# Block kernel on one core: merge loads moved into the SSM stage, the experts' end worked by 128-row blocks with four extra load areas, and the RWKV shift split into single operations

## The chip, the cores and the metric

The program runs on one core of one Trainium2 chip. The time is device microseconds from the start to the end of one execution. Before the change three runs gave a median of 5053.02 us (5052.44 to 5054.24). All arithmetic is fp32.

## What is computed

The reference is a stack of blocks on 512 tokens of width 1024. The first one mixes two branches and is followed by a mixture of experts; two attention blocks come after it. Cut to what matters here:

```python
pl = hl @ w_in; rw, ss, gates = split(pl)          # also for 256 context tokens
ya = rwkv_branch(centred_shift(rw))                # u + mu0*(prev-u) + mu1*(next-u), then two scans
yb = ssm_branch(to_colmajor(ss))                   # conv, two chunked scans, rms_norm over 2048
ga, gb = split(sigmoid(gates))
m  = (ga * (ya @ proj_a) + gb * (yb @ proj_b)) @ w_out
x  = x + g1 * rms_norm(m)
h2 = rms_norm(x) * (1 + sc2) + sh2
x  = x + g2 * rms_norm(ec_moe(h2))                 # 16 experts, each takes its 64 best tokens
for l in range(2):                                 # attention, gates, FFN; first line of each:
    h = rms_norm(x, attn_norm[l]); proj = h @ w_in_2[l]
```

## The kernel before, in words

The program is a row of stages: start, RWKV, SSM, merge, experts (MoE), and two attention blocks (block2). In each stage every engine has its own function (`..._sync` for SP, which issues all DMAs on one queue, `..._tensor` for TensorE, `..._vector`, `..._scalar`, `..._gpsimd`). Engines run in program order and wait for one another by counting semaphores. At a stage's end each engine calls `meet` (L211): it drains, counts up its own line, and waits for the lines of all four compute engines.

**RWKV** works on 8 tiles of 128 channels (j = 0 to 7). What the engines do is set by one list, `b.order`, that `rwkv_order` (L672) makes: eight generators are asked in turn (`turns`, L371), once each in a round, and what they yield is written one behind the other: two lanes (d = 0, 1: triangular inverses of one scan direction each, 16 rounds for two chunks: `tri`, then five `level`/`merge` pairs with `products` between them, `turn_bk`, `corner`, `join`), two steppers (`rest`, `solve`, `update`), the tails, the projector, the chain (decay factors and keys), the modulator. Each engine walks this list and does its share of each step. A lane takes 48 rounds for a tile. The projector yields for tile j: 8 `project` steps for k (i = 1), `shift` steps, 2 `lora` steps, 8 `project` steps for r (i = 2), a `shift` step, `kk_norm`, 8 `project` steps for v (i = 0), `shift` steps, `turn_v` (six transposes), `gate`, 2 `lora` steps. In a `shift` step (L1121) ScalarE first scales the PSUM result in full at part 0 (`shift`, L1338), and VectorE then adds the left and the right neighbour with one `scalar_tensor_tensor` each: two operations for columns 0 to 512 in part 0, two for 512 to 768 (the context) in part 1. In the `corner` step TensorE's result is copied by VectorE (two copies for each lane) and by ScalarE (one), and `join` on TensorE waits for these copies. VectorE's predicated copies of the next `tri` wait for GpSimd to have filled X (`unit`, L1467), and GpSimd's keys stand ahead of that in its order.

**SSM** (`ssm_order`, L1503) ends with 16 `mgate` steps (merge gates: eight matmul pairs each, copied by ScalarE, stored to `gmd` by SP); the tiles of yb go to `ybd` from the `read` steps. Its last work is `yrstd`: VectorE, ScalarE, VectorE, four small matmuls, one copy; then `meet`.

**Merge** (`merge_sync`, L2013): SP waits for the meeting, then loads in order pa 0, yaT (2 MB, from `yad`), pb 0, ybT (4 MB, from `ybd`), gates, pa 1, pb 1 and the rest. TensorE takes pa d and pb d in turn for d = 0 to 7 (8 and 16 matmuls of 128x512, two records each), then the output projection. Weights go through a ring of six areas of 1 MB in `wreg`.

**Experts** (`moe_sync`, L2173): 192 loads of 1 MB through a ring of eight areas, two for each step of the list `todo`; the load for step i waits until TensorE has finished step i - 4. After the last `combine(7)` VectorE adds four 128-row blocks, ScalarE squares all four, VectorE makes one `mvar` for all, ScalarE one Ln and Exp for all, VectorE scales and adds the four blocks; `meet`; then block2 starts with its norm of x (square, variance, Ln, Exp, scale, eight transposes, gain, for each block) and meets once more (`("norm", 0)`). SP issues c2 and the first two weights of block2 (b0a) after the first of these meetings.

## Time and profile before

| | |
|---|---|
| median of 3 runs | 5053.02 us |
| the profiled execution | 5058.15 us |
| its span in the trace | 5056.1 us |
| PE busy / PE weight loads / DVE / ACT / POOL | 91% / 56% / 41% / 26% / 9% |
| granted TensorE clock, mean | 0.954 |
| DMA | 503 MB, mean 100 GB/s; 351 to 408 GB/s in the experts' slices |
| stages in the trace (us) | RWKV 53 to 1214, SSM to 1975, merge to 2225, experts to 2808, block2 to the end |

The busy share of PE is modelled (a matmul's end is not seen), so it says that PE seldom waits, not that it runs at its peak. In rows of the timeline the first number is the start, the second the time from the first to the last of the merged instructions, the brackets tell how long the engine had been idle and what released it. PEclk is the granted clock as a share of 2.4 GHz.

### The profile page before, as it was taken

To read this page: it belongs to the slowest core of one execution; us is meant where nothing else is said; L and a number is where in the kernel's file an instruction comes from. 1 tells how busy PE (TensorE), PEld (TensorE's weight loads), DVE (VectorE), ACT (ScalarE), POOL (GpSimd) and SP (SyncE) were. 2 spreads that over 40 slices of the span, in tenths; PEclk is the share of its full clock that TensorE was granted. 3 is DMA by queue.
4 is the path that set the end of the run, shared out by engine and by line. 5 is a ranking of instruction groups with operands and counts; after the bars stand their busy time and mean duration, and the time that the engine had idled before them with its cause. 6 is when DMAs were issued, how large, how long until landed. Compare 5 with 4: busy or idle time off the path is not lost.

```text
span 5056.1 us, 85351 instructions
## 1 busy us (share of the span) xinstructions
PE 4614.6 (91%) x36404; PEld 2842.8 (56%) x36404; DVE 2087.9 (41%) x3866; ACT 1336.7 (26%) x2486; POOL 431.0 (9%) x385
## 2 busy tenths in 40 slices
PE   7899899988998898979998898989999998999999
PEld 3566666666555553464443544544788544444787
DVE  3554555463355542130111336463343237463333
ACT  2333333332222211010000124251232123242232
POOL 0121111110222230000000000020000000020000
PEclk9998999998999999989999899999999999999999
DMA  6200000000111014318998211013321211113321
GB/s 228 81 19 5 18 19 17 5 26 13 42 46 38 34 73 179 118 76 351 407 408 362 97 62 61 35 59 140 115 86 50 87 62 61 43 56 139 113 100 50
DMA packets 76818, 503.33 MB, mean 100 GB/s; under 512 B 9480, under 2 KB 10008, under 8 KB 34328
## 3 DMA queue, kind: packets, MB, share of 16 engines
q1 hardware_dynamic: 76440, 497.88, 25.6%
q8 instruction: 287, 4.70, 0.4%
q14 instruction: 91, 0.75, 0.0%
HBM read 472.66 MB, written 25.19 MB: 98 GB/s over the span
## 4 chain that ended last, share of the span: by engine, by line
PE 79%; DVE 8%; issue 6%; DMA 3%; ACT 2%; POOL 1%; SPq 0%; PEldq 0%; PEld 0%; DVEq 0%; ACTq 0%; POOLq 0%
PE ps L224 76%; PE ps L227 3%; DMA upper<-in_ew 2%; DVE upper L243 2%; ACT upper L282 2%; DVE upper L259 1%; DVE upper L235 1%; POOL upper L3394 1%; DVE upper L251 1%; DVE lower L235 1%; DVE lower L243 1%; ACT lower L282 0%; DVE upper L239 0%; DMA upper<-ybd 0%; DVE lower L239 0%
## 5 line engine op out<-in xcount | busy, mean ns | idle before, releaser
L224 PE MATMUL ps<-lower 128*128 128x512 f32 (+12 forms) x7024 | 1935.6, 444 | 66.5 <-issue 22.8
L224 PEld LDWEIGHTS ps<-lower 128*128 128x128 f32 (+3 forms) x7024 | 958.9, 188 | 782.8 <-issue 610.0
L224 PE MATMUL ps<-upper 64*64 64x64 f32 (+7 forms) x15552 | 829.9, 258 | 144.3 <-DVE upper L251 46.4
L282 ACT ACTIVATE upper<-ps 128x512 f32<-128x512 f32 (+5 forms) x967 | 444.9, 491 | 1769.1 <-PE ps L224 1300.8
L224 PEld LDWEIGHTS ps<-upper 64*64 64x64 f32 (+4 forms) x15552 | 596.9, 145 | 449.7 <-issue 223.8
L224 PE MATMUL ps<-lower,upper 64*64 64x64 f32 (+6 forms) x7536 | 725.3, 316 | 50.5 <-DMA lower<-in_ada 20.3
L224 PE MATMUL ps<-rounded 128*128 128x512 f32 x3072 | 712.3, 394 | 7.5 <-DVEq L213 7.5
L224 PEld LDWEIGHTS ps<-rounded 128*128 128x128 f32 x3072 | 579.6, 189 | 139.4 <-issue 8.3
L224 PEld LDWEIGHTS ps<-lower,upper 64*64 64x64 f32 (+3 forms) x7536 | 384.3, 145 | 337.8 <-issue 267.1
L282 ACT ACTIVATE upper<-upper 128x256 f32<-128x256 f32 (+12 forms) x695 | 361.9, 529 | 725.1 <-DVE upper L255 186.8
L224 PE MATMUL ps<-upper,lower 128*128 128x512 f32 (+4 forms) x1584 | 482.1, 474 | 26.2 <-DMA upper<-yad 11.7
L224 PEld LDWEIGHTS ps<-upper,lower 128*128 128x128 f32 (+1 forms) x1584 | 248.3, 197 | 248.9 <-issue 230.0
L259 DVE COPY_PREDICATED upper<-lower,ps 128x256 f32<-128x256 uint8 (+2 forms) x576 | 246.2, 457 | 328.6 <-PE ps L224 293.0
L251 DVE COPY upper<-ps 128x64 f32<-128x64 f32 (+9 forms) x423 | 166.8, 404 | 454.0 <-PE ps L224 423.6
L235 DVE TENSOR_TENSOR rounded<-lower,rounded 128x512 fp32r<-128x512 f32 (+2 forms) x136 | 200.8, 1477 | 226.6 <-ACT rounded L282 226.4
L235 DVE TENSOR_TENSOR upper<-upper,ps 128x512 f32<-128x512 f32 (+1 forms) x136 | 108.5, 798 | 450.2 <-PE ps L224 437.2
L282 ACT ACTIVATE rounded<-lower 128x512 fp32r<-128x512 f32 (+2 forms) x136 | 171.7, 1262 | 374.5 <-PE ps L224 239.7
L227 PE MATMUL ps<-lower,upper 128*128 128x128 f32 (+1 forms) x1204 | 189.0, 290 | 83.6 <-ACT upper L282 38.7
L227 PEld LDWEIGHTS ps<-lower,upper 128*128 128x128 f32 (+1 forms) x1204 | 145.3, 147 | 176.3 <-issue 73.6
L282 ACT ACTIVATE lower<-ps 128x512 f32<-128x512 f32 (+1 forms) x174 | 102.2, 592 | 381.2 <-PE ps L224 351.5
L243 DVE SCALAR_TENSOR_TENSOR upper<-ps,lower,upper 128x511 f32<-128x511 f32 (+1 forms) x208 | 130.1, 625 | 134.1 <-ACT upper L282 128.4
L3381 POOL COPY upper<-lower 128x512 f32<-128x512 f32 x8 | 5.0, 631 | 1933.2 <-PE ps L224 1932.5
(81 smaller groups left out, 2139.5 us busy)
## 6 DMA issues: line engine op xcount, KB each, us to landing
lower<-in_ew SPq DMA_DIRECT2D x144, 1024.0 KB, 10.6
upper<-in_ew SPq DMA_DIRECT2D x48, 1024.0 KB, 13.6
lower<-in_b0f SPq DMA_DIRECT2D x16, 2048.0 KB, 8.0
lower<-in_b1f SPq DMA_DIRECT2D x16, 2048.0 KB, 7.9
upper<-in_ada SPq DMA_DIRECT2D x18, 1024.0 KB, 5.4
lower<-in_wrkv SPq DMA_DIRECT2D x8, 1728.0 KB, 7.5
lower<-in_b0g SPq DMA_DIRECT2D x8, 1536.0 KB, 6.7
gad<-upper SPq DMA_DIRECT2D x48, 256.0 KB, 2.0
```

Source lines behind the costliest of these rows:

```text
L224: return self.e.matmul(out, lhsT, rhs, start=start, stop=stop)
L227: return self.e.transpose(out, in_, self.ident[0:n, 0:n])
L235: self.e.tensor_tensor(out, a, b, op).then_inc(line.up(*event), 1)
L243: self.e.scalar_tensor_tensor(out, a, s, b, op0, op1).then_inc(line.up(*event), 1)
L251: self.e.tensor_copy(out, a).then_inc(line.up(*event), 1)
L259: self.e.copy_predicated(out, mask, data).then_inc(line.up(*event), 1)
L282: self.e.activation(out, in_, func, bias=bias, scale=scale, accum_out=accum).then_inc(line.up(*event), 1)
L3381: g.e.tensor_copy(b3[:, :, 0:64], v3(b.kv[:, i, :], 128)[:, :, 0:64]).then_inc(tail.pool.up(), 1)
L3394: g.e.tensor_tensor(y, y, r, SUB).then_inc(o.lane.pool.up("less", *o.u), 1)
```

## The change

Three parts. In the **RWKV** order a `shift` step is one operation of VectorE, so the projector yields 4, 2 and 4 of them where it yielded 2, 1 and 2. In the **merge** the loads for its start are issued from the SSM stage: yaT right after the stores of SSM group 2 (into group 0's memory, which is then free), pa 0 and pa 1 after merge gate 11, pa 2 and pb 0 after gate 15. TensorE leaves the SSM stage without waiting for the others, and takes pa 0, 1, 2, pb 0, pa 3, pb 1, pa 4, ... (`MERGE`). In the **experts** four loads (steps 4 and 5 of `todo`) go into areas that only later hold acc and r1, r2, r3, scr; the two row loads r2, r3 move behind step 11's load; the last blocks' norm is taken in a staggered order by blocks of 128 rows, block2's first norm with it; the meeting `("norm", 0)` goes; block2's first two weights are issued once step 93 of `todo` is done, ahead of the meeting, and c2 behind it.

```diff
@@ rwkv_order, projector
-                    for part in range(2):
+                    for part in range(4):
                         yield once(("shift", j, i, part))
...
-            yield once(("shift", j, 2, 0))
+            for part in range(2):
+                yield once(("shift", j, 2, part))
...
-            for part in range(2):
+            for part in range(4):
                 yield once(("shift", j, 0, part))
@@ rwkv_vector
-            s, e = ((0, 512), (512, 768))[part]
+            s, e = ((0, 512), (512, 768))[part // 2]
             v.wait_ge(P.act, "project", j, i)
...
+            if part % 2 == 0:
+                v.stt(P.dve, out[:, s + 1:e], ps[:, s:e - 1], ...)
+            else:
+                v.stt(P.dve, out[:, s:e - 1], ps[:, s + 1:e], ..., *last)
@@ ssm_sync
+            if name != "mgate" or z[0] < 11:
+                k.ring.load(*next(k.loads))
+            elif z[0] == 11:
+                merge_begin(k, sp)
+                merge_load(k)
+                merge_load(k)
+            else:
+                merge_load(k)
+                merge_load(k)
...
+            if z == [2, 7]:
+                sp.wait_ge(k.tail.act, "square", 2, 3)
+                for line in k.stored:
+                    sp.wait_ge(line)
+                fetch(sp, k.mg.yaT, k.yad.rearrange("k p t -> p k t"), "yaT")
@@ ssm_tensor
-    pe.meet("pe", "ssm")
+    banks.give("yrstd", M.dve, "rb")
+    k.free = free
+    pe.leave("pe", "ssm")
@@ merge
+MERGE = [("pa", 0), ("pa", 1), ("pa", 2)] + [t for d in range(8) for t in ([("pb", d), ("pa", d + 3)] if d < 5 else [("pb", d)])]
@@ moe_sync
+    ring, extra = Ring(sp, b.w, k.wline[4:8] + k.wline[0:4]), Ring(sp, b.extra, [k.line(f"extra{i}") for i in range(4)])
...
-        if i == 4:
+        if i == 12:
+            sp.wait_ge(M.pe, *todo[5])
             fetch(sp, b.r2, k.mrow_bc(5120, 1024), "r2")
             fetch(sp, b.r3, k.row("n2post"), "r3")
...
+            (extra if i in (4, 5) else ring).load(
+                (*key, e), T[name][2 * (2 * g + e) + f][:, 2048 * z:2048 * z + 2048], M.pe, *key)
+    sp.wait_ge(M.pe, *todo[93])
@@ moe_vector, after the last "down"
+    for t in range(9):
+        if t < 4:
+            combine(7, (t,))
+        if 0 <= t - 2 < 4:
+            add(t - 2)
+        if 0 <= t - 4 < 4:
+            norm_scale_vector(k, v, "attn0", t - 4, b.nscr, b.nss)
+        if 0 <= t - 1 < 4:
+            var(t - 1)
+        if 0 <= t - 3 < 4:
+            norm_var_vector(k, v, "attn0", t - 3, b.nss)
+        if 0 <= t - 5:
+            norm_turn_vector(k, v, "attn0", t - 5, ...)
@@ moe_scalar
+    for t in range(7):
+        if t < 4:
+            a.wait_ge(M.dve, "combine", 7, t)
+            a.act(M.act, b.scr, b.acc[:, t, :], AF.Square, "msq", t, accum=b.ss[:, t:t + 1])
+        if 0 <= t - 1 < 4:
+            r = b.ss[:, t - 1:t]
+            a.wait_ge(M.dve, "mvar", t - 1)
+            a.act(M.act, r, r, AF.Ln)
+            a.act(M.act, r, r, AF.Exp, "mrstd", t - 1, scale=-0.5)
+        if 0 <= t - 2 < 4:
+            a.wait_ge(M.dve, "x1", t - 2)
+            norm_square_scalar(k, a, "attn0", t - 2, b.nscr, b.nss)
+        if 0 <= t - 3:
+            norm_rstd_scalar(k, a, "attn0", t - 3, b.nss)
```

**VectorE at the first corner of a tile.** The lanes are at tile 4, the projector at tile 5, i = 0 (v): 128x511 and 128x255 are the shift's operations, the 128x768 one behind it is the chain's `beta`, the COPY rows are the four corner copies, TENSOR_SCALAR 128x768 is the chain's `keys`, COPY_PREDICATED the masks of `tri` and of the next `merge`. Before:

```order
L243 SCALAR_TENSOR_TENSOR upper<-ps,lower,upper 128x511 x2
L243 SCALAR_TENSOR_TENSOR upper<-lower,upper 128x768
L251 COPY upper<-ps 64x256
L251 COPY upper<-ps 64x4x64
L251 COPY upper<-ps 64x256
L251 COPY upper<-ps 64x4x64
L243 SCALAR_TENSOR_TENSOR upper<-ps,lower,upper 128x255 x2
L239 TENSOR_SCALAR upper<-upper,lower 128x768
L259 COPY_PREDICATED upper<-lower,ps 128x256 x8
```

Now:

```order
L247 SCALAR_TENSOR_TENSOR upper<-ps,lower,upper 128x511
L247 SCALAR_TENSOR_TENSOR lower<-lower,upper 128x768
L255 COPY upper<-ps 64x256
L255 COPY upper<-ps 64x4x64
L255 COPY upper<-ps 64x256
L255 COPY upper<-ps 64x4x64
L247 SCALAR_TENSOR_TENSOR upper<-ps,lower,upper 128x511
L243 TENSOR_SCALAR upper<-upper,lower 128x768
L247 SCALAR_TENSOR_TENSOR upper<-ps,lower,upper 128x255
L263 COPY_PREDICATED upper<-lower,ps 128x256 x6
L247 SCALAR_TENSOR_TENSOR upper<-ps,lower,upper 128x255
L263 COPY_PREDICATED upper<-lower,ps 128x256 x2
```

One operation of 128x511 moved from ahead of the corner copies to behind them, and the last of 128x255 behind the copies of `tri`.

**TensorE at the same place.** Its rows begin with the `join` of both lanes (the last 8 of the 64x64 x9), then `turn_v` (128x128 x6), `tri` of both lanes (64x64 and 128x128 out of lower), `rest`, `gate` (128x512), and the next `level`. Before:

```order
L224 MATMUL ps<-upper 64x64 x9
L227 MATMUL ps<-lower,upper 128x128 x6
L224 MATMUL ps<-lower 64x64 x8
L224 MATMUL ps<-lower 128x128 x4
L224 MATMUL ps<-lower 64x64 x8
L224 MATMUL ps<-lower 128x128 x4
L224 MATMUL ps<-upper 64x64 x8
L224 MATMUL ps<-lower 128x512
L224 MATMUL ps<-upper 64x64 x4
```

Now (the row x12 is `rest` and the first four of `level`; x8 the last of `level` and `solve`):

```order
L228 MATMUL ps<-upper 64x64 x9
L228 MATMUL ps<-lower 64x64 x8
L228 MATMUL ps<-lower 128x128 x4
L228 MATMUL ps<-lower 64x64 x8
L228 MATMUL ps<-lower 128x128 x4
L228 MATMUL ps<-upper 64x64 x12
...
L228 MATMUL ps<-upper 64x64 x8
L231 MATMUL ps<-lower,upper 128x128 x6
L228 MATMUL ps<-upper 64x64 x16
L228 MATMUL ps<-upper 64x128 x8
L228 MATMUL ps<-lower 128x512
```

`turn_v` and `gate` moved from ahead of the next `level` to behind it.

**SP from the last merge gates to the start of the merge.** Before (the meeting is what pa's load waits for):

```order
L1595 DMA gmd<-upper 128x512 [waits proj_act] x2
L337 DMA lower<-in_pa 128x1024 [waits end_act,end_pool,end_dve,end_pe]
L471 DMA upper<-yad 128x8x512 [waits stored1,stored0]
L337 DMA lower<-in_pb 128x2048 [waits kept1,kept0]
L471 DMA upper<-ybd 128x16x512
L2033 DMA lower<-gmd 128x512
```

Now (yaT and the first two pa stand further up, among the gates' stores):

```order
L1606 DMA gmd<-upper 128x512 [waits proj_act] x2
L342 DMA lower<-in_pa 128x1024
L342 DMA lower<-in_pb 128x2048
L476 DMA upper<-ybd 128x16x512 [waits stored0,stored1,end_pool,kept0,end_act,kept1,end_dve,end_pe]
L2070 DMA lower<-gmd 128x512
```

Of the start's loads only ybT still waits for the meeting.

## Rows read from the trace of the kernel before

**Rows 1.** Busy time by stretches, RWKV and merge: stretch, length, engines, clock, DMA

```profile
core 0: us, PE busy (x) PEld busy (x) DVE busy (x) ACT busy (x) POOL busy (x), PEclk, DMA share, GB/s
53.00:1214.00 1161.00, 1035.64 (x20320) 734.85 (x20318) 597.11 (x1310) 418.17 (x795) 173.50 (x169) 0.92 0.08 29
...
1975.00:2225.00 250.00, 224.22 (x640) 122.56 (x640) 45.91 (x59) 24.93 (x50) 0.00 (x0) 0.96 0.35 128
```

**Rows 2.** Timeline, end of SSM to start of merge, PE and SP

```profile
1962.49 7.13 PE L224 MATMUL ps<-lower 128*128 128x512 f32 x16 [1.12 <-ACT upper L282]
...
1972.37 1.93 PE L224 MATMUL ps<-lower 128*128 128x128 f32 x8 [2.75 <-DVE lower L239]
...
1976.95 0.53 SPq L471 DMA_DIRECT2D upper<-ybd  x1
...
1986.04 8.86 PE L224 MATMUL ps<-upper,lower 128*128 128x512 f32 x16 [11.74 <-DMA upper<-yad]
```

**Rows 3.** Timeline of the merge, PE and DVE each

```profile
1999.40 159.87 PE L224 MATMUL ps<-upper,lower 128*128 128x512 f32 x368 [4.50 <-DMA upper<-ybd]
...
2013.64 1.23 DVE L235 TENSOR_TENSOR lower<-lower,upper 128x1024 f32<-128x1024 f32 x1 [38.29 <-DMA upper<-in_prow]
```

**Rows 4.** Experts, first group: SP's and PE's timeline, one stretch of 5 us

```profile
2306.16 0.80 SPq L337 DMA_DIRECT2D upper<-in_ew  x2
2332.42 7.69 SPq L337 DMA_DIRECT2D lower<-in_ew  x6
...
2302.47 3.65 PE L224 MATMUL ps<-upper 128*64 128x512 f32 x16 [1.30 <-DMA upper<-in_ew]
...
2325.00:2330.00 5.00, 5.00 (x16) 2.58 (x18) 0.33 (x2) 0.00 (x0) 0.00 (x0) 0.50 0.00 0
```

**Rows 5.** Timelines from the experts' end to block2: DVE, ACT, PE

```profile
2773.50 1.22 DVE L235 TENSOR_TENSOR upper<-upper,ps 128x1024 f32<-128x1024 f32 x1 [2.14 <-PE ps L224]
...
2783.29 1.28 DVE L243 SCALAR_TENSOR_TENSOR upper<-upper 128x1024 f32<-128x1024 f32 x1 [1.79 <-ACT upper L282]
...
2795.74 0.75 DVE L239 TENSOR_SCALAR lower<-lower 128x1024 f32<-128x1024 f32 x1 [0.50 <-ACT lower L282]
...
2774.75 1.06 ACT L282 ACTIVATE upper<-upper 128x1024 f32<-128x1024 f32 x1 [19.65 <-DVE upper L235]
...
2781.52 1.28 ACT L278 ACT_TABLE_LOAD   x1 [0.47 <-DVE upper L239]
2782.82 0.44 ACT L282 ACTIVATE upper<-upper 128x4 f32<-128x4 f32 x2
...
2807.75 42.43 PE L224 MATMUL ps<-lower 128*128 128x384 f32 x124 [1.51 <-POOLq L213]
```

**Rows 6.** What PE waited for, RWKV from 150 us on: total, times, longest

```profile
PE ps L224 <- DVE upper L251: 43.3, 23, 3.6
```

**Rows 7.** Timelines of one first corner (lanes at tile 4): DVE, POOL, PE

```profile
755.40 1.53 DVE L243 SCALAR_TENSOR_TENSOR upper<-ps,lower,upper 128x511 f32<-128x511 f32 x2 [1.02 <-ACT upper L282]
...
766.00 2.69 DVE L259 COPY_PREDICATED upper<-lower,ps 128x256 f32<-128x256 uint8 x6 [4.62 <-POOL upper L1467]
...
761.46 1.54 POOL L1298 TENSOR_TENSOR upper<-lower,upper 128x768 f32<-128x768 f32 x1 [1.59 <-DVE upper L239]
...
758.90 1.97 PE L224 MATMUL ps<-upper 64*64 64x64 f32 x16 [3.58 <-DVE upper L251]
760.80 1.54 PE L227 MATMUL ps<-lower,upper 128*128 128x128 f32 x6
...
765.75 1.12 PE L224 MATMUL ps<-lower 128*128 128x512 f32 x2
767.45 0.34 PE L224 MATMUL ps<-upper 64*64 64x64 f32 x8 [0.58 <-DVE upper L259]
```

**Rows 8.** Busy time in stretches of 4 us behind a first and a second corner

```profile
758.00:762.00 4.00, 3.10 (x22) 2.92 (x22) 3.21 (x7) 0.76 (x2) 2.35 (x2) 0.50 0.01 4
...
810.00:814.00 4.00, 4.00 (x53) 3.16 (x53) 1.48 (x4) 0.90 (x1) 0.00 (x0) 0.50 0.00 0
```

**Rows 9.** Timeline of ACT: Ln and Exp of `kk_rstd`

```profile
846.37 1.72 ACT L282 ACTIVATE upper<-upper 128x768 f32<-128x768 f32 x2 [5.00 <-DVE upper L239]
```

More of the change, by code:

```diff
@@ L209, in wait_ge, with leave @@
             self.e.wait_ge(line.sem, count)
+    def leave(self, mine, stage):
+        self.e.drain().then_inc(self.k.end[mine].up(stage), 1)
     def meet(self, mine, stage):
-        self.e.drain().then_inc(self.k.end[mine].up(stage), 1)
+        self.leave(mine, stage)
         for e in self.k.end:
@@ L727, in chain @@
                 if d == 0:
-                    yield from until("shift", j, 1, 1)
+                    yield from until("shift", j, 1, 3)
                     yield once(("kk_square", j))
@@ L1484, in ssm_map @@
     b.groups = []
-    for _ in range(2):
+    for z in range(2):
         o = Bag()
+        if z == 0:
+            at = m.top
+        else:
+            b.third = (at, m.top)
         o.bcm, o.ccm, o.btok = m(768), m(512), m(768)
@@ L2007, in merge_map @@
     sa = [m(512)]
-    b.x, b.mT, b.yaT, b.ybT = v3(m(4096), 1024), v3(m(4096), 512), v3(m(4096), 512), v3(m(8192), 512)
+    b.x = v3(m(4096), 1024)
+    assert k.ss.third[0] <= m.top and m.top + 4096 <= k.ss.third[1]
+    b.yaT, b.mT, b.ybT = v3(m(4096), 512), v3(m(4096), 512), v3(m(8192), 512)
     sa.append(m(512))
@@ L2017, in merge_map, with merge_begin, merge_load @@
     return b
+MERGE = [("pa", 0), ("pa", 1), ("pa", 2)] + [t for d in range(8) for t in ([("pb", d), ("pa", d + 3)] if d < 5 else [("pb", d)])]
+def merge_begin(k, sp):
+    areas = [k.wreg[:, 2048 * i:2048 * i + 2048] for i in (2, 3, 0, 1, 4, 5)]
+    k.ring = Ring(sp, areas, k.wline[2:8])
+    k.loads = iter([((name, d), k.T[name][d], k.main.pe, "branch", d, int(name == "pb")) for name, d in MERGE] +
+                   [(("wo", n), k.T["wo"][n], k.main.pe, "out", 3) for n in range(4)])
+def merge_load(k):
+    k.ring.load(*next(k.loads))
 def merge_sync(k, sp):
@@ L2023, in merge_sync @@
         sp.wait_ge(k.end[e], "ssm")
-    ring = Ring(sp, [k.wreg[:, 2048 * i:2048 * i + 2048] for i in range(6)])
-    def load(name, d):
-        ring.load((name, d), T[name][d], M.pe, "branch", d, 1)
     def gates(d):
@@ L2053, in merge_sync @@
     fetch(sp, b.n2s, k.mrow_bc(3072, 1024), "n2s")
[L2054 to L2059 removed]
+    for t, (name, d) in enumerate(MERGE[6:] + [("wo", n) for n in range(4)]):
+        merge_load(k)
+        if t % 2 and t // 2 + 2 < 8:
+            gates(t // 2 + 2)
 def merge_tensor(k, pe):
     b, M = k.mg, k.main
[L2064 to L2075 removed]
+    banks = Banks(pe, 0, 8, k.free)
+    for name, d in MERGE:
+        br, src, source = ((0, b.yaT, "yaT"), (1, b.ybT, "ybT"))[name == "pb"]
+        w, loaded = k.slot[name, d]
+        w = v3(w, 128)
+        ps = banks.take(("branch", d, br))
+        pe.wait_ge(loaded, name, d)
+        pe.wait_ge(k.line(source), source)
+        nk = 8 * (br + 1)
+        for kk in range(nk):
+            last = pe.mm(ps, w[:, kk, :], src[:, kk, :], kk == 0, kk == nk - 1)
+        last.then_inc(M.pe.up("branch", d, br), 1)
+        banks.give(("branch", d, br), M.dve, "branch", d, br)
     for i in range(4):
@@ L2296, in moe_tensor @@
     combine(7)
+    for i in range(4):
+        norm_turn_tensor(k, pe, banks, "attn0", i, b.nscr)
     pe.meet("pe", "moe")
@@ L2334, in gather, with combine @@
         v.copy(M.dve, b.XE[g % 3][:, 4:8, :], v3(k.pair(("gather", g))[:, 512:1024], 128), "gather", g)
-    def combine(g):
-        for i in range(4):
+    def combine(g, rows=range(4)):
+        for i in rows:
             ps = k.pair(("combine", g, i))
@@ L2645, in block2_sync @@
     b, T, M, P = k.b2[l], k.T, k.main, k.proj
-    top = "moe" if l == 0 else ("block2", 0)
-    for e in k.end:
-        sp.wait_ge(k.end[e], top)
-    if l == 0:
-        fetch(sp, k.c2b, T["c2"], "c2")
+    if l:
+        for e in k.end:
+            sp.wait_ge(k.end[e], ("block2", 0))
     ring = Ring(sp, [k.wreg[:, 4096 * i:4096 * i + 4096] for i in range(2)])
@@ L2662, in block2_sync @@
     ring.load(*next(loads))
+    if l == 0:
+        for e in k.end:
+            sp.wait_ge(k.end[e], "moe")
+        fetch(sp, k.c2b, T["c2"], "c2")
     for g, name in zip(b.gains, ("aqn", "akn", "bqn", "bkn")):
@@ L2738, in block2_tensor @@
     at = {}
-    if l == 0:
-        for i in range(4):
-            norm_turn_tensor(k, pe, whole, "attn0", i, b.nscr)
-        pe.meet("pe", ("norm", l))
     def dense(name, t, i, s, width):
@@ L3205, in block2_scalar @@
     b, M, P, tail = k.b2[l], k.main, k.proj, k.tail
-    if l == 0:
-        for i in range(4):
-            norm_rows_scalar(k, a, "attn0", i, b.nscr, b.nss)
-        a.meet("act", ("norm", l))
     def dense(name, t, i, s, dst, width):
@@ L3371, in block2_gpsimd @@
     b, M, tail = k.b2[l], k.main, k.tail
-    if l == 0:
-        g.meet("pool", ("norm", l))
     for name, *z in b.order:
```

117 lines of the change are left out of this document (46 added, 71 removed).

## The prediction

> **What bounds the kernel now.** I read the busy time by stretches first: it tells which stage belongs to which engine. In RWKV (1161 us) TensorE is busy for 1035.64 and in the merge for 224.22 of 250 [rows 1]; VectorE has half of the one and a fifth of the other. So an edit pays by what it takes out of TensorE's idle time, or by the work it ends earlier. The timelines then show where that idle time lies. Between SSM and merge TensorE waits 11.74 us for yaT and later 4.50 us for ybT [rows 2, 3]; behind that come 368 records without a gap. In the experts' first group it waits once, for 1.30 us [rows 4]; behind the last `down` it does nothing until block2 begins at 2807.75, while VectorE and ScalarE take turns [rows 5]. In RWKV the sum of the waits for the corner copies is 43.3 us in 23 [rows 6], and one corner in detail is in [rows 7].
>
> **The merge's start.** Removed: the meeting ahead of yaT and of pa's first two loads. They now land while the last gates run. TensorE ends `yrstd` at 1972.37 + 1.93 = 1974.30 [rows 2] and can begin pa0 there. Nothing else feeds it: its banks have been given back, and VectorE's first work in the merge, which waited for in_prow until 2013.64 [rows 3], is not needed until the banks are full. A record of the merge takes 159.87/368 = 0.434 us [rows 3], so the 384 records of this stretch take 166.8, and end at 1974.4 + 166.8 = 2141.2 instead of 1999.40 + 159.87 = 2159.3: **−18.1 us**. What must hold: ybT still waits for the meeting. Its issue stands at 1976.95 [rows 2], and everything queued with it (0.5 MB of pa, 2 of yaT, 1 of pb, 4 of ybT) had landed at 1999.40 [rows 3], which is 7.5 MB in 22.5 us, 334 GB/s. Its own 4 MB at that speed land near 1989.5. The three pa now ahead of pb0 keep TensorE until 1974.4 + 48 x 0.434 = 1995.2, so some 6 us are left. If ybT took as long as in the trace of before (1999.4), 4.2 us would come back; the term lies between −13.9 and −18.1. I take −18.1, since the trace's time had the other loads in it. Past the moved loads, SP's queue has the gates' stores, which no engine waits for.
>
> **Four loads ahead in the experts.** TensorE waits 1.30 us at 2302.47 [rows 4] for a weight that now comes sooner: **−1.3**. More is not in it. SP issues two loads at 2306.16, and the next only at 2332.42; between 2325 and 2330 the DMA queues move 0 GB/s and TensorE runs without a gap at a clock of 0.50 [rows 4]. The four loads thus move 4 MB into a time in which the queues stand still anyway. If none of that idle time swallowed them, 4 MB at the 334 GB/s above, some 12 us less the 1.3 counted, would be saved as well; so 0 to −11 beside the −1.3, and I take 0, because the idle stretch is wider than the head start. The two small loads r2 and r3 move into the same stretch.
>
> **The experts' end.** From the first `combine` (2773.50) to block2 (2807.75) is 34.25 us [rows 5]. Before, all four blocks went through each step, and each turn of VectorE and ScalarE waited for the other. Now the blocks are one step apart. VectorE's own work is 4 `combine` of 1.22, 4 adds of 1.28 and 4 second steps of the same kind, 4 scalings of 0.75 [rows 5] and 4 turns of about the length of a `combine`, with the small ones some 24 us. What remains of waits for ScalarE: one table load of 1.28, a square of 1.06 and Ln/Exp of 0.44 ahead of the first block's return [rows 5], and the last block's own square and rstd. Laid out by hand, the last turn ends near 2802.1 instead of 2807.5: **−5.4**. Bounds: 24 us with no wait left would be −10; with Ln and Square in different tables and a load for each change (up to 3 more of 1.28), −1.6. I take the schedule. The row shows 1.28 us for the table load and Ln starting 1.30 us after it (2781.52, 2782.82) [rows 5]. The Trainium skill ("ScalarE: Activation LUTs", What ACT_TABLE_LOAD costs) adds a drain of some 1.38 us to each load; by that, as an estimate, the end would gain 4.0. The trace shows no such gap, and decides.
>
> **RWKV's shifts.** Nothing is added or removed: the `stt` of a tile's three shifts are the same, issued one a step, and a tile keeps its 48 steps. Of the 23 waits, eleven are about 3.55 us (3.58 in [rows 7]), 39 of the 43.3 us; they fall where a shift of i = 0 (six) or i = 1 (five) lies ahead of the corner copies. In the new order nine of these still meet a shift (tiles 3 to 7 with i = 0, 4 to 7 with i = 1), with one operation of it ahead instead of two: 1.53/2 = 0.77 us less each [rows 7].
> At i = 1 that is a plain gain, 4 x −0.77 = −3.1. At i = 0 it is not. There TensorE waits next for the masks, which wait for GpSimd, which waits for `keys2` at 761.46 and so for VectorE's `keys` [rows 7]. That chain comes only about 1 us earlier, while `turn_v` (1.54, of which about 0.8 are of the start) and `gate` (1.12), which filled TensorE's time ahead of it, have moved behind it [rows 7]: 0.77 gained, about 1.6 to 2 of cover lost, net +0.85, over five tiles +4.3. So there are two shorter idle times in place of one. Behind such a wait the clock is at 0.50 for 4 us and more [rows 8]; a second idle time holds it there longer, at 0 to 3 us a tile, and I take 1: +5.
> The third corner: `kk_rstd` (1.72 on ScalarE [rows 9]) now stands ahead of that engine's corner copies; half of it shows, 0.8 x 5 = +4. In tile 1 two corners are freed of a shift. A corner without one waits (43.3 − 39)/12 = 0.36, so each gives at most 3.2; I take 2.75 each, −5.5, with −6 for the low clock that goes with them and +1.5 for one corner that gets a shift. Sum: −3.1 + 4.3 + 5 + 4 − 5.5 − 6 + 1.5 = **about 0**, with bounds of −20 (all of the low clock behind the nine goes) and +15 (it lasts longer at each). It is the least certain term.
> [...]
>
> **The sum.** −18.1 − 1.3 − 5.4 + 0 = −24.8. The profiled execution took 5058.15; it would be 5033.3. The median of the runs shown is 5.1 lower, 5053.0, so the forecast is **5028 us**. A difference of 0.2%, 10.1 us, is about what a measurement of this kernel tells from none: faster is under 5042.9, slower over 5063.1.
>
> **The rivals.**
> *RWKV gains.* Less work ahead of the copies turns the waits short enough for the clock to stay up. For it: nine waits shrink, and two go. Against it: at the first corner the wait only moves. From 9 x 0.77 + 2 x 3.2 = 13 to twice that with the clock: 5002 to 5015. Chance 0.17.
> *RWKV costs.* The second idle time at the first corner grows to 2.5 us, and the clock stays at 0.50 through it: 3 us more at each of five tiles, 5043. For it: [rows 7] show nothing else that TensorE could do there. Against it: GpSimd may run ahead by more than I reckon. Chance 0.17.
> *The head start in the experts stays.* The idle stretch of the queues shrinks less than the loads gain: 9 us more, 5019. Chance 0.06.
> *The merge waits for ybT all the same.* It lands as late as before, or VectorE's loads of in_prow come later behind it and fill the banks: 8 us of the 18 return, 5036. Chance 0.05.
> *Slower.* At the third corner `kk_rstd` delays the ScalarE copies by its 1.72 and the clock drops behind it in every tile, where the trace of before has no drop at that corner. Half the speed over 4 us costs 2, over 8 us 4, so at most some 6 us in each of six tiles, 36: 5064. It decides from (24.8 + 10.1)/6 = 5.8 us a tile on. Against it: the waits left over from the eleven are short. Chance 0.04.
> *The change doesn't do what it says* is in the forecast for one part: the four loads ahead bring almost nothing.
>
> **How the numbers follow.** The forecast, with RWKV within 8 us of nothing and the end of the experts within its bounds, has 0.51 and spans 5020 to 5036. The range takes in the smaller gain of RWKV below and the costly first corner above: 5010 to 5045; outside are the upper half of RWKV's gain, and slower. Faster by over 0.2%: all of the forecast and the gaining cases, and three fifths of the costly one (its middle lies at the edge, 5042.9, and its smaller sizes are the likelier): 0.79 + 0.10 = 0.89. Within 0.2%: 0.07. Slower: 0.04.
>
> **What would show it.** In the new profile TensorE's first record of the merge at the end of `yrstd`, with no wait for yaT and none for ybT in 384 records; block2 some 29 us behind the first `combine`; the load waits of the experts' first group gone, and SP's gap still there; in RWKV a sum of corner waits of 30 to 35 us in place of 43.3, and a new wait for GpSimd's or VectorE's masks of 2 to 3 us at the first corners. Wrong it would be if RWKV's length moved by more than 8 us either way, or if a wait for ybT or for a bank stood in the merge.

## The result and the profile after

The changed kernel takes **5017.69 us** (median of 4 runs, 5013.05 to 5023.26) against 5053.63 for the kernel before (4 runs); the ratio is 0.9928, with a 95% interval of 0.9916 to 0.9940. That is 0.72% faster, 36 us. The forecast was 25 us; 5017.7 lies in the stated range (5010 to 5045), but below the 5020 to 5036 that the forecast itself was to span. The profiled execution's span is 5020.2 us (5056.1 before): 35.9 less.

Cut at the same instructions in both traces, the span divides as follows (us). `yrstd` is counted from its first matmul; "the last combine" is TensorE's part of it, which begins 2 us ahead of VectorE's first `combine`.

```
stage                                        before     after   difference
start to RWKV's end (SSM's first record)     1217.73   1208.51    -9.22
SSM to yrstd                                  754.64    751.66    -2.98
yrstd to pa0                                   13.67      2.19   -11.48
pa0 to the first record of "out"              174.93    167.26    -7.67
out, router, to the first expert's record     114.20    116.29    +2.09
experts to the last combine                   496.33    496.69    +0.36
last combine to block2's first record          36.25     30.36    -5.89
block2 to the end                            2248.35   2247.24    -1.11
```

**The merge.** The PE timeline of the changed kernel, and SP's:

```profile
1960.17 1.93 PE L228 MATMUL ps<-lower 128*128 128x128 f32 x8 [2.76 <-DVE lower L243]
1962.36 165.71 PE L228 MATMUL ps<-upper,lower 128*128 128x512 f32 x384 [0.26 <-issue]
2129.62 5.63 PE L228 MATMUL ps<-lower,upper 128*128 128x256 f32 x25 [1.55 <-DVE upper L239]
```

```profile
1922.96 0.93 SPq L342 DMA_DIRECT2D lower<-in_pa  x2
...
1958.87 0.44 SPq L342 DMA_DIRECT2D lower<-in_pa  x1
...
1963.29 0.38 SPq L476 DMA_DIRECT2D upper<-ybd  x1
```

The 11.74 and the 4.50 us of [rows 2, 3] are gone: all 384 records stand in one row, which starts 0.26 us behind `yrstd`, and ybT, issued at 1963.29, kept nobody waiting.

**The experts.** SP's timeline of the first group: it still issues nothing from 2277 to 2299.91, as from 2306.16 to 2332.42 in [rows 4].

```profile
2275.28 0.80 SPq L342 DMA_DIRECT2D upper<-in_ew  x2
...
2276.62 0.43 SPq L476 DMA_DIRECT2D upper<-in_prow  x1
2299.91 7.69 SPq L342 DMA_DIRECT2D lower<-in_ew  x6
```

**The experts' end.** VectorE's, ScalarE's and TensorE's timelines, against [rows 5]:

```profile
2744.59 1.22 DVE L239 TENSOR_TENSOR upper<-upper,ps 128x1024 f32<-128x1024 f32 x1 [0.78 <-PE ps L228]
...
2750.49 1.28 DVE L247 SCALAR_TENSOR_TENSOR upper<-upper 128x1024 f32<-128x1024 f32 x1 [1.25 <-ACT upper L286]
...
2770.26 2.55 DVE L239 TENSOR_TENSOR lower<-ps,lower 128x1024 f32<-128x1024 f32 x2
```

```profile
2748.73 1.28 ACT L282 ACT_TABLE_LOAD   x1
2750.02 1.59 ACT L286 ACTIVATE upper<-upper 128x1 f32<-128x1 f32 x3
```

```profile
2772.96 63.71 PE L228 MATMUL ps<-lower 128*128 128x384 f32 x192 [1.66 <-DVEq L213]
```

From the first `combine` to block2 it is now 28.37 us instead of 34.25. One table load remains, and Ln starts 1.29 us after it began: again nothing stands between the load and Ln.

**RWKV.** A tile has three corners. In the later tiles the shift of i = 0 stands near the first, that of i = 1 near the second and that of i = 2 near the third. What TensorE waited for from 150 us on (total, times, longest), in place of the 43.3 us in 23 of [rows 6] (L255 are the corner copies, L263 the masks). The first row is the masks' row before, the others are of the changed kernel:

```profile
PE ps L224 <- DVE upper L259: 31.4, 48, 1.6
...
PE ps L228 <- DVE upper L263: 42.7, 59, 2.7
PE ps L228 <- DVE upper L255: 30.6, 24, 2.8
...
PE ps L231 <- DVE upper L263: 9.2, 11, 1.3
```

The corners cost 12.7 us less, and the masks 11.3 more in the one row and about 5 more in the other (9.2 us; 3.9 before). So the waits as a whole did not shrink. What shrank is TensorE's busy time for the same work: from 53 us to SSM's first record it is 1023.56 us now and was 1035.64, while its idle time went from 129.1 to 132.0 (mean clock 0.92 before, 0.93 now). One period, from a third corner to a second one, TensorE's waits (the lanes at tile 4):

```profile
693.18 1.27 PE L231 MATMUL ps<-lower,upper 128*128 128x128 f32 x8 [1.25 <-DVE upper L263]
...
741.81 1.86 PE L228 MATMUL ps<-upper 64*64 64x64 f32 x15 [2.79 <-DVE upper L255]
750.12 0.49 PE L228 MATMUL ps<-upper 64*64 64x64 f32 x8 [1.92 <-DVE upper L263]
...
790.85 0.67 PE L228 MATMUL ps<-upper 64*64 64x64 f32 x8 [2.77 <-DVE upper L255]
```

The first corner's wait is 2.79 instead of 3.58 [rows 7], and behind it stands one wait of 1.92 for the masks, where the trace of before has two, of 0.58 [rows 7] and 0.60. The second corner's is 2.77 instead of 3.55. The 1.25 us ahead of the third corner are new; VectorE's timeline shows why:

```profile
692.02 0.75 DVE L247 SCALAR_TENSOR_TENSOR lower<-ps,lower 128x511 f32<-128x511 f32 x1 [2.03 <-ACT lower L286]
692.69 0.77 DVE L263 COPY_PREDICATED upper<-lower,ps 128x256 f32<-128x256 uint8 x2
```

VectorE stood 2.03 us at the shift of i = 2, which needs ScalarE's projection, with the masks queued behind. A tile takes 136.5 us, as before (136.6). It is measured between GpSimd's mask copies at two third corners: 697.93 and 834.44 now, 717.32 and 853.94 before. In it TensorE is idle for 1.0 us more and busy for 1.1 us less:

```profile
717.32:853.94 136.62, 123.44 (x2478) 88.83 (x2474) 70.46 (x157) 51.80 (x100) 23.73 (x23) 0.91 0.05 17
697.93:834.44 136.51, 122.36 (x2478) 87.42 (x2474) 70.22 (x157) 52.09 (x99) 23.71 (x23) 0.92 0.05 17
```

### The profile page after: what moved, and what is told of

The parts are those of the page before. It is cut to its first block, busy times and chain, and to the rows that moved or that the text cites. A ratio compares the mean times of both kernels' runs of the same rounds, so it can differ in the third digit from the quotient of the medians.

```text
span 5020.2 us, 85352 instructions
## 1 busy us (share of the span) xinstructions
PE 4595.0 (92%) x36404; PEld 2831.8 (56%) x36404; DVE 2086.9 (42%) x3869; ACT 1338.8 (27%) x2490; POOL 431.0 (9%) x385
## 4 chain that ended last, share of the span: by engine, by line
PE 79%; DVE 8%; issue 6%; DMA 2%; ACT 2%; POOL 1%; SPq 0%; PEldq 0%; PEld 0%; DVEq 0%; ACTq 0%; POOLq 0%
PE ps L228 76%; PE ps L231 3%; DMA upper<-in_ew 2%; DVE upper L263 2%; ACT upper L286 2%; DVE upper L247 1%; DVE upper L239 1%; POOL upper L3461 1%; DVE upper L255 1%; DVE lower L239 1%; DVE upper L243 1%; ACT lower L286 0%; DVE lower L247 0%; DVE lower L243 0%; DMA lower<-in_ada 0%
## 5 line engine op out<-in xcount | busy, mean ns | idle before, releaser
L228 PE MATMUL ps<-upper 64*64 64x64 f32 (+8 forms) x15584 | 836.4, 259 | 145.2 <-DVE upper L263 38.7
L228 PE MATMUL ps<-lower,upper 64*64 64x64 f32 (+6 forms) x7504 | 714.4, 313 | 51.7 <-DMA lower<-in_ada 20.9
L286 ACT ACTIVATE upper<-upper 128x512 f32<-128x512 f32 (+9 forms) x709 | 364.7, 523 | 723.7 <-DVE upper L259 186.1
L263 DVE COPY_PREDICATED upper<-lower,ps 128x256 f32<-128x256 uint8 (+2 forms) x576 | 245.7, 457 | 287.0 <-PE ps L228 257.2
L255 DVE COPY upper<-ps 128x64 f32<-128x64 f32 (+9 forms) x423 | 166.8, 405 | 435.0 <-PE ps L228 393.5
```

The lines of the kernel that those rows point to most:

```text
L228: return self.e.matmul(out, lhsT, rhs, start=start, stop=stop)
L255: self.e.tensor_copy(out, a).then_inc(line.up(*event), 1)
L263: self.e.copy_predicated(out, mask, data).then_inc(line.up(*event), 1)
L286: self.e.activation(out, in_, func, bias=bias, scale=scale, accum_out=accum).then_inc(line.up(*event), 1)
```

## The experiments

Executions of one kernel spread by 10 us and more, so verdicts on a stage are read from the stage's length in the trace. There is one trace for each run, and stages of unchanged code differ between traces too (the old RWKV order takes 1211.93 to 1217.73 us in three traces). The stages of all runs:

```
run                 ratio to before (95%)      RWKV     SSM   pa0..out  experts   end
before              1                        1217.73  754.64   174.93   496.33   36.25
after               0.9928 (0.9916-0.9940)   1208.51  751.66   167.26   496.69   30.36
rwkv                0.9989 (0.9979-0.9998)   1205.55  754.32   174.93   496.12   36.24
merge               0.9961 (0.9948-0.9974)   1211.93  753.76   167.23   494.60   36.24
experts             0.9981 (0.9972-0.9989)   1216.75  754.87   174.94   494.78   30.98
noextra             0.9939 (0.9927-0.9951)   1209.52  749.14   167.28   496.40   30.35
i1_late             0.9918 (0.9904-0.9931)   1205.90  749.70   167.26   492.73   30.35
i0_late             0.9971 (0.9961-0.9982)   1222.68  754.50   167.27   496.40   30.34
tile12              0.9926 (0.9911-0.9941)   1205.68  749.07   167.28   493.78   30.98
split_i1            0.9961 (0.9949-0.9974)   1227.47  753.87   167.24   492.95   30.35
place               0.9934 (0.9921-0.9946)   1207.20  753.96   167.24   494.23   30.82
dodge1              0.9879 (0.9863-0.9895)   1179.01  749.53   167.26   497.38   30.96
dodge2              0.9861 (0.9845-0.9878)   1172.71  749.60   167.27   494.50   30.69
pause               0.9911 (0.9896-0.9925)   1190.76  754.35   167.24   492.73   30.36
```

RWKV divided at GpSimd's mask copies: up to tile 1, tile 1, tiles 2 to 5 with TensorE's busy time and mean clock in them, and what is left (tiles 6 and 7 and the end):

```
run         to tile 1  tile 1  tiles 2-5   busy  clock    rest
before         297.81  145.31     547.40  496.05  0.91  227.21
merge          297.96  140.00     545.70  495.26  0.91  228.27
experts        303.61  140.20     545.95  494.55  0.91  226.99
rwkv           293.79  128.89     547.95  492.05  0.92  234.92
after          294.10  128.91     548.45  492.19  0.92  237.05
noextra        295.20  129.20     548.97  492.43  0.92  236.15
i1_late        296.00  129.06     549.33  496.65  0.92  231.51
i0_late        297.01  136.42     560.73  505.81  0.90  228.52
tile12         289.87  136.31     550.02  498.52  0.91  229.48
split_i1       310.74  138.63     546.54  494.27  0.92  231.56
place          300.17  133.16     545.61  493.50  0.92  228.26
dodge1         298.10  133.28     517.15  475.03  0.95  230.48
dodge2         295.29  133.25     515.49  470.00  0.97  228.68
pause          289.25  128.90     538.80  488.17  0.94  233.81
```

**rwkv: the shifts alone.** The diff's hunks of `rwkv_order` and `rwkv_vector` on the kernel before.

> The kernel before with the RWKV part alone (shifts one operation a step). Theory from the two traces: its stage ends 9.2 us earlier, of that about 17 won in tile 1 (two corners freed of a shift, and the low clock behind them), nothing in tiles 3 to 7 (a loss at the first corner and a gain at the second cancel), and about 8 lost in the last tile, which has the first corner's loss without the second's gain: 9 us faster than before. Rival: the SSM stage, 3 us shorter in the changed trace, belongs to this part too: 12 us faster. Rival from the prediction: nothing, within 3 us of before.

Measured: 5050.51 us beside 5056.11, 1 to 11 us faster; the RWKV stage 1205.6 us, the SSM stage 754.3. So the 3 us of SSM don't belong to this part. "Nothing" (within 3 us) is not ruled out by the whole kernel's interval; the stages speak against it. The old order took 1211.93, 1216.75 and 1217.73 us in three traces, the new one 1205.55, 1208.51 and 1209.52 in three (this run, the changed kernel, noextra). The distance of the middle ones is 8 us, and the nearest two are 2.4 apart.

**merge: the merge part alone.**

> The kernel before with the merge part alone (yaT and the first loads during SSM, no meeting). Theory: TensorE starts pa0 right behind yrstd and runs 384 records without a gap, 18 to 19 us faster than before. Rival: the moved loads change the SSM stage too, 21 to 22 us faster. Rival of the prediction: ybT is late, 14 us or less.

Measured: 5037.00 us, 13 to 26 us faster. pa0 to `out` is 167.23, to 0.03 as in the changed kernel, `yrstd` to pa0 2.21: 19.2 us less, with the SSM stage at 753.8. Its RWKV stage, whose code is the one before, took 1211.93 us: 5.8 less than in the trace of before. The stretch from `out` to the experts is 116.28 here too and 114.20 wherever the merge is the old one: 2.1 us are given back in the router, every time. TensorE's router work, the 32 transposes and the 64 matmuls of 128x16, takes longer, behind the same idle time of 8.95 us. First the changed kernel, then the one before:

```profile
2194.06 6.20 PE L231 MATMUL ps<-lower 128*128 128x128 f32 x32 [8.95 <-DVEq L213]
2201.55 12.80 PE L228 MATMUL ps<-upper,lower 128*128 128x16 f32 x64 [1.28 <-ACT lower L286]
```

```profile
2225.42 5.19 PE L227 MATMUL ps<-lower 128*128 128x128 f32 x32 [8.95 <-DVEq L213]
2232.43 11.16 PE L224 MATMUL ps<-upper,lower 128*128 128x16 f32 x64 [1.83 <-ACT lower L282]
```

That is 1.0 and 1.6 us more, less 0.55 of a shorter wait. The granted clock is lower there: 0.54 and 0.80 in the two stretches of 5 us from 2194.62 on, against 0.75 and 0.94 in the same ones before (from 2225.97 on). Why the clock comes back later behind the same idle time was not found out.

**experts: loads ahead and the end by blocks.**

> The kernel before with both expert edits (four loads ahead, and the end by blocks of 128 rows). Theory: the stretch from the last combine's start to block2 goes from 34.25 to about 28.5 us, and the loads ahead bring nothing over the stage: 5.5 to 7 us faster than before. Rival: the head start of four loads is kept where the stage does not begin 30 us earlier: 14 us faster.

Measured: 5046.51 us, 5.5 to 14 faster; the end 30.98 for 36.25, the stage 494.8 for 496.3. The rival's 14 us are at the interval's end; the trace shows 5.3 us at the end and 1.5 in the stage.

**noextra: the changed kernel without the four loads ahead.**

```
-            (extra if i in (4, 5) else ring).load(
+            ring.load(
...
+    ring.i = 4
...
-        if i == 12:
-            sp.wait_ge(M.pe, *todo[5])
+        if i == 4:
```

> The changed kernel without the four loads ahead (eight areas instead of twelve, all else as changed). Theory: the queues stand still for some 10 us in the first group in both, and the stage is bound by its loads afterwards; within 1.5 us of the changed kernel. Rival: the loads ahead are worth their waits, 4 to 9 us slower than the changed kernel.

Measured: 5024.71 us, ratio 0.9939 (0.9927 to 0.9951) against 0.9928 (0.9916 to 0.9940). The middles are 5 to 6 us apart, as the rival has it, and the intervals overlap, so the whole kernel's time decides nothing here. The stage itself takes 496.40 us against 496.69. SP's timeline in the first group:

```profile
2275.28 0.81 SPq L342 DMA_DIRECT2D upper<-in_ew  x2
2301.54 7.70 SPq L342 DMA_DIRECT2D lower<-in_ew  x6
```

SP issues nothing from 2276.1 to 2301.5 us, and with four loads more nothing from 2277.0 to 2299.9. The head start is spent there. Over all traces the stage takes 492.7 to 497.4 us with the four loads (ten traces, 494.6 on average) and 494.6 to 496.4 without them (four, 495.9 on average). The difference of 1.3 us is smaller than the spread.

**i1_late, i0_late, tile12: which split costs.** The changed kernel with a condition on the tile j and on i; where it is false, the shift goes in pairs as before:

```
+def SPLIT(j, i):
+    return j <= 2 or i == 1      # i0_late: j <= 2 or i == 0; tile12: j <= 2
...
-                    for part in range(4):
+                    for part in range(4 if SPLIT(j, i) else 2):
```

> The changed kernel, but from tile 3 on only the shifts of i = 1 are split (i = 0 and 2 in pairs as before). Theory: in tiles 3 to 7 the split of i = 0 costs 3.5 to 5.6 us a tile (a second wait for the masks at the first corner) and that of i = 1 gives 5.7 back at the second. Without the first, the RWKV stage is 17 to 28 us shorter than the changed kernel's 1208.5, and the kernel 17 to 28 us faster than it. Rival: both corners share one cause and the gain at the second follows from the shape of the first; then within 5 us of the changed kernel.

> The changed kernel, but from tile 3 on only the shifts of i = 0 are split. Theory: it keeps the cost at the first corner and loses the gain of 5.7 us at four second corners: RWKV stage near 1231, 23 us longer than the changed kernel's. Rival: within 5 us of the changed kernel.

> The changed kernel, but from tile 3 on all shifts are in pairs as before; only the first three tiles' shifts are split. Theory: the two parts that cancel in the later tiles are both gone, the win of tile 1 (about 15 us from the corners freed of a shift) stays, and so does the last tile's loss avoided: RWKV stage 1200 to 1205, 3 to 8 us shorter than the changed kernel's 1208.5. Rival: the win does not come from tile 1, and the stage is as before, 1212 to 1218.

Measured RWKV stages: 1205.9, 1222.7 and 1205.7. So i1_late is 2.6 us shorter than the changed kernel, where 17 to 28 were expected; i0_late is 14.2 us longer, where 23 were expected; tile12 is as expected to 1 us, but not for the expected reason. The split of i = 0 does cost: alone it makes tiles 2 to 5 13 us longer (560.7 against 547.4). Of these, 9.8 are TensorE's busy time for the same matmuls, at a mean clock of 0.90. But that of i = 1 brings nothing by itself: a tile takes 136.5 us in i1_late (701.20 to 837.74) as in tile12 (136.3). My theory of two parts that cancel fell. The parts do not even add: beside the split of i = 0, those of i = 1 and 2 bring 12 us (560.7 to the changed kernel's 548.5). Why was not found out. In tile12 tile 1 takes 136.3 us, as in i0_late, and not the 129 of the runs in which tile 3's shift of i = 1 is split as well: part of tile 1's gain hangs on that shift. TensorE and VectorE in i1_late, ahead of the third corner, show where the gain goes:

```profile
695.09 1.85 PE L228 MATMUL ps<-upper,lower 128*128 128x512 f32 x4 [1.69 <-DVE lower L247]
```

```profile
693.50 1.54 DVE L247 SCALAR_TENSOR_TENSOR lower<-ps,lower 128x511 f32<-128x511 f32 x2 [2.02 <-ACT lower L286]
694.95 0.76 DVE L263 COPY_PREDICATED upper<-lower,ps 128x256 f32<-128x256 uint8 x2
```

```profile
692.00:696.00 4.00, 2.02 (x50) 1.23 (x43) 2.18 (x4) 1.31 (x3) 0.00 (x0) 1.00 0.01 2
696.00:700.00 4.00, 4.00 (x14) 2.89 (x13) 1.24 (x2) 2.00 (x3) 0.00 (x0) 0.57 0.02 4
```

The two steps that i = 1 takes more move everything behind it in the projector by two. The projection of i = 2 then ends so late that its shift waits for ScalarE, with the masks queued behind it: TensorE waits 1.69 us, and the clock is 0.57 in the four microseconds after.

**split_i1: i = 1 split in all tiles, the others nowhere.**

> The changed kernel with the split of i = 1 alone in all tiles. In the order the shifts of tile 2 (i = 0) and tile 3 (i = 1) then meet a corner of tile 1 again. Theory: as the run with i = 1 split from tile 3 on, less the two freed corners of tile 1, so 5 to 14 us longer than that run. Rival: the place of the shifts in tile 1 does not matter; within 2 us of that run.

Measured: RWKV 1227.5 us, 21.6 longer than i1_late, more than the 5 to 14 expected. 15 of these are there at tile 0's second mask copies (223.65 against 208.74), where this order puts the work of the beginning otherwise; what delays it was not looked into. 8.7 come in the stretch that was in question, from tile 1's second corner to tile 2's first (100.9 us against 92.2), which is the size expected. So the place in tile 1 matters, and the split of i = 1 alone is no way to have it.

**pause: i1_late with one empty step ahead of the shift of i = 2.**

```
+            if j > 2:
+                yield None
             for part in range(2 if SPLIT(j, 2) else 1):
                 yield once(("shift", j, 2, part))
```

> The run with i = 1 split from tile 3 on, and one empty step ahead of the shifts of i = 2. Theory: there the gain at the second corner was given back at the third, where the shift of i = 2 waited 2 us for ScalarE's projection with the masks of the next merge queued behind it (a wait of 1.69 us for TensorE and a low clock behind it). One step later it has nothing to wait for and no masks behind it: 2 to 4 us a tile, RWKV stage 10 to 20 us shorter than the 1205.9 of that run. Rival: kk_rstd, one step later as well, delays ScalarE's corner copies instead: within 3 us of that run.

Measured: RWKV 1190.8, 15.1 less than i1_late. The expected 10 to 20 are met only by luck: 6.9 of these were there at the first mask copies, which the pause can't touch, so 8 are its own. A tile takes 134.0 us, 2.6 less, and the wait of 1.69 is 0.76, while those at the first and second corner are unchanged (3.57 and 2.77). So this much of the giving back at the third corner is shown: it is that shift with the masks behind it. By the ratios (0.9911 against 0.9918 for i1_late, with intervals that overlap) nothing can be told.

**place: pairs as before, and two shifts moved one step.**

```
+                    for _ in range(int(j == 3)):
+                        yield None                # ahead of the shifts of i = 1
...
+            for _ in range(int(j == 2)):
+                yield None                        # ahead of the shifts of i = 0
```

> The changed kernel with all shifts in pairs again, as before, and one empty step of the projector ahead of the shifts of i = 0 in tile 2 and of i = 1 in tile 3, so that both stand behind tile 1's corner copies instead of ahead. Theory: what tile 1 gains in the changed kernel (13 to 17 us from its second to its third mask copies) comes from the place of these shifts alone: the same gain here, RWKV stage 1200 to 1206, kernel 5005 to 5015. Rival: the splitting itself brings it, then the stage is 1212 to 1218 as before.

Measured: RWKV 1207.2 us and 5022.99 in all, both longer than expected. Tile 1, from GpSimd's mask copies at its start to those at its end, takes 145.3 us in the trace of before (297.81 to 443.12), and in the two others with the old order 140.0 (merge) and 140.2 (experts); the changed kernel takes 128.9, and this one 133.2. So the place of the two shifts brings 7 of the changed kernel's 11 us, less than the 13 to 17 that I expected: I had compared with the trace of before alone, which is slow in just this stretch (TensorE is busy for 134.0 us in it, and for 129.0 and 128.4 in the two others). The three runs with both shifts moved agree on this tile: 133.2 to 133.3.

**dodge1, dodge2: all shifts behind the corners.** As place, with `int(j > 2)` empty steps ahead of i = 1 (dodge1), and two ahead of i = 0 from tile 3 on (dodge2).

> As the run with two empty steps, and one more empty step ahead of the shifts of i = 1 in tiles 4 to 7, which moves the whole pair behind the second corner's copies. Theory: the second corner's wait falls from 3.55 to 1 us or less and the low clock behind it goes, 3 to 5 us in each of four tiles, since the pair is 1.53 of it and ScalarE's projection, which it waits for, another 1; RWKV stage 12 to 20 us shorter than in that run. Rival: the work behind the corner waits for the later shift or the later i = 2, and gives it all back, as the split did; within 3 us of that run.

> As the last, and two empty steps ahead of the shifts of i = 0 in tiles 3 to 7: they stand behind the first corner's copies and behind keys. Theory: the first corner's wait falls from 3.57 to about 1 us, but TensorE meets the masks sooner, with turn_v and gate moved behind: their wait grows from 1.2 to 3 us or more; sum within 1 us a tile, so within 5 us of the last run. Rival: keys come 1.5 us earlier and the low clock goes: 10 us or more shorter.

Measured: RWKV 1179.0 and 1172.7 us, 4993.45 and 4986.26 us in all. dodge1's stage is 28 us shorter than place's, where 12 to 20 were expected: 7.1 us a tile over tiles 2 to 5. TensorE at the second corner of dodge1, and the clock there, against 3.55 us and 0.50 before [rows 8]; the first row is TensorE's of the kernel before:

```profile
805.40 1.97 PE L224 MATMUL ps<-upper 64*64 64x64 f32 x16 [3.55 <-DVE upper L251]
...
775.13 0.67 PE L228 MATMUL ps<-upper 64*64 64x64 f32 x8 [0.50 <-DVE upper L255]
```

```profile
775.00:779.00 4.00, 3.66 (x76) 3.18 (x78) 3.72 (x8) 1.70 (x5) 0.11 (x1) 1.00 0.03 6
```

GpSimd's mask copies at two third corners, one tile apart, in dodge1:

```profile
689.35 0.87 POOL L1483 COPY upper<-lower 128x256 f32<-128x256 f32 x2 [31.84 <-PE ps L228]
...
818.93 0.87 POOL L1483 COPY upper<-lower 128x256 f32<-128x256 f32 x2 [31.85 <-PE ps L228]
```

A tile takes 129.6 us instead of 136.6. The wait is 3.05 us shorter, and TensorE's busy time for the same 2478 matmuls falls by 4.2 us, from 123.44 to 119.28, with the mean clock at 0.95 instead of 0.91: behind the corner it is at the upper of its two levels (2.4 GHz) instead of the lower.

```profile
689.35:818.93 129.58, 119.28 (x2478) 85.58 (x2474) 71.08 (x157) 51.88 (x100) 23.76 (x22) 0.95 0.06 18
```

Both corners of dodge2, and the clock behind the first:

```profile
723.99 0.67 PE L228 MATMUL ps<-upper 64*64 64x64 f32 x8 [0.90 <-DVE upper L255]
731.53 0.49 PE L228 MATMUL ps<-upper 64*64 64x64 f32 x8 [3.48 <-DVE upper L263]
...
770.52 0.67 PE L228 MATMUL ps<-upper 64*64 64x64 f32 x8 [0.50 <-DVE upper L255]
```

```profile
732.00:736.00 4.00, 3.84 (x80) 3.42 (x74) 1.59 (x4) 1.75 (x4) 0.09 (x1) 0.50 0.02 4
```

At the first corner the wait moves to the masks, from 0.58 and 0.60 to 3.48, as expected. Over tiles 2 to 5 dodge2 is only 1.7 us shorter than dodge1, and 2.8 of the stage's 6.3 us were there before tile 1, which its edit doesn't touch; by the ratios (0.9879 and 0.9861, intervals that overlap) the two can't be told apart. **Both beat both kernels**: their whole intervals (0.9863 to 0.9895 and 0.9845 to 0.9878) lie below the changed kernel's, with the same matmuls and the same pairs of shifts as before.

## Why the prediction came out as it did

The direction and the range held, and three of four terms to 2 us. The fourth, RWKV, was mis-sized, and the forecast's own sign of being wrong, a move of RWKV's length by more than 8 us, fired in this pair of traces (9.2). Term by term, in the profiled executions:

- **The merge's start: −18.1 forecast, −19.15 measured** (11.48 + 7.67), and in the run of it alone 19.2. The steps of the working held: TensorE starts at `yrstd`'s end, a record takes 165.71/384 = 0.432 us where 0.434 was reckoned (1 us over 384 records), ybT has room. Not foreseen were the 2.1 us that come back in the router, in all eleven runs with the new merge; net 17.1.
- **Four loads ahead: −1.3 forecast, +0.4 measured.** The one wait of [rows 4] is gone, but the stage took 492.7 to 497.4 us whatever was ahead, so a gain of 1.3 us can neither be seen nor denied. The reading that the idle queues swallow the head start is borne out by the run without it.
- **The experts' end: −5.4 forecast, −5.9 measured**, 5.3 to 5.9 in all runs.
- **RWKV: about 0 forecast, −9.2 measured** in this trace; with the spread of 1211.9 to 1217.7 for the old order the part is worth 2 to 12 us in the traces and 1 to 11 by the run alone. This is the term that was mis-sized. The preamble and tile 0 were put at nothing and gained 3.7 (mask copies at 297.81, now 294.10); the traces spread by more than that there (295.3 to 303.6 with the shifts in pairs there, 289.3 to 297.0 with all of them split). Tile 1 was put at −5.5 − 6 + 1.5 = −10, and gained 16.4 (145.3 to 128.9); 11.2 against the two other traces of the old order, so that the size was good and 5 of the 6 us too few belong to the one execution that it was compared with. For the later tiles a loss of 10.2 was forecast, and 10.9 were measured. That agreement is luck: the forecast spreads the loss evenly, about 1.9 us for each of four tiles and 2.7 for the last, and the traces have +1.0 in all of tiles 2 to 5 and +9.8 in the rest. In that rest TensorE's waits are the same (41.8 and 41.9 us) and its busy time is not (184.40 and 194.10).
- **SSM: −3.0**, which no term had. No part of the change makes it alone: each part's run has about 754 us. Of the ten traces of the changed kernel and its variants six take 749 to 752 us and four about 754. The cause is open.

Inside the later tiles the waits came nearly as reckoned, and the clock did not. At the first corner the corner's wait is 2.79 and the masks' 1.92, for an estimate of 2 to 3. The price at the third corner was put on `kk_rstd` ahead of ScalarE's copies; the runs i1_late and pause show another one: the shift of i = 2 ahead of the masks. The clock's share is where the working failed. For the later tiles it took 1 us a tile at the first corner and nothing at the second and third. These stretches show the clock behind each corner: at the first from 758.90 (before) and 741.81 (after), at the second 805.40 (before), 790.85 and 927.32 (after):

```profile
758.90:772.90 14.00, 12.83 (x284) 10.37 (x286) 7.07 (x19) 5.44 (x13) 8.40 (x9) 0.81 0.01 2
741.81:755.81 14.00, 11.90 (x200) 10.21 (x200) 5.67 (x13) 3.76 (x9) 7.32 (x8) 0.51 0.01 2
...
805.40:817.40 12.00, 12.00 (x120) 8.62 (x124) 7.17 (x14) 3.75 (x7) 0.00 (x0) 0.58 0.00 1
790.85:802.85 12.00, 11.79 (x260) 9.96 (x260) 7.29 (x13) 4.92 (x10) 0.00 (x0) 0.86 0.02 4
927.32:939.32 12.00, 11.98 (x208) 10.14 (x210) 5.75 (x12) 4.66 (x10) 0.00 (x0) 0.63 0.01 1
```

In these tiles the first corner lost clock and the second gained some, 0.28 in one tile and 0.05 in the next, behind waits of the same length (2.77 and 2.76). The third has lost some too: 0.57 from 830 to 834, where the trace of before has 1.00 from 846 to 854. And ahead of the first corner, where the clock was 0.50 from 746 to 750 before, it is 1.00 from 730 to 738 now. When the second corner's wait goes almost entirely (dodge1), the busy time falls by 4.2 us a tile, more than the 3.05 us of the wait. The measured time, 5017.7, lies between the forecast's 5020 to 5036 and the 5002 to 5015 of the rival "RWKV gains". That rival's condition, waits short enough for the clock to stay up, is met only in part by halving what stands ahead of the corner; moving it behind meets it.

The Trainium skill ("TensorE: Matmul & The Clock Gate", A second HAM failure mode: psum-queue depth-cycling) tells of another kernel, in which TensorE stands idle for a moment between groups of matmuls so often that its clock goes down and up and throughput is lost. This case agrees in so far as the split of i = 0 alone (i0_late), which makes two waits of 2.79 and 1.92 us at the first corner, costs 9.8 us of busy time over four tiles. The second corner's wait of 0.50 us in dodge1 leaves the clock at 1.00.

## What to carry to other kernels

Where one engine's queue is shared by a critical chain and by side work, ask first at which step the side work stands against the chain's short, waited-for operations: moving it behind them made this stage 33 to 39 us shorter (dodge1) and 39 to 45 (dodge2), by which trace of the old order one takes. Cutting it into smaller steps brought 2 to 12, in part because the extra steps pushed something else ahead of the next such operation. Count a wait of TensorE with the clock that it costs behind it. Here a wait shortened by a fifth kept part of that price, and one cut to half a microsecond kept none. And compare a stage with more than one trace of the unchanged code before a difference of 5 us is given a cause.

## What the runs showed of the hardware

Taking 3.05 us from a wait of 3.55 us made a tile 7 us shorter; the granted clock behind the corner went from 0.50 to 1.00. Waits of 2.77 us still brought a lower clock, and by different amounts: 0.86 over 12 us behind one of them and 0.63 behind the next, a tile later in the same trace.

A stage's length differs from trace to trace by some 5 us with the same code: RWKV's old order took 1211.93 to 1217.73 us. SSM shows two lengths (749.1 to 751.7, and 753.8 to 754.9), with the same number of operations on every compute engine (TensorE's matmuls are 3312 in each of the fourteen traces). And with a merge that starts 11 us sooner behind SSM the router takes 2.1 us more at a lower clock, in all eleven runs.
